# Gathering a third of the first one-hots from an identity matrix, and preparing the next stage's tiles inside the stage before it

## The reference, cut to what matters

```python
q = jnp.einsum('pd,de->pe', tb, wq).reshape(-1, PEER_HEADS, 2, half)
s = jnp.einsum('phik,hink->phin', q, subkeys).astype(jnp.float32)
s1, i1 = lax.top_k(s[:, :, 0], PEER_TOPK)
s2, i2 = lax.top_k(s[:, :, 1], PEER_TOPK)
...
gate = jax.nn.softmax(top_s, axis=-1)
ue = jnp.take(table_u, idx, axis=0)
ve = jnp.take(table_v, idx, axis=0)
act = jax.nn.gelu(jnp.einsum('pd,phkd->phk', tb, ue).astype(jnp.float32), approximate=False)
return jnp.einsum('phk,phkd->pd', (gate * act).astype(tb.dtype), ve)
```

## Time and profile before

| what | us |
|---|---|
| median of three runs | 3470.91 |
| profiled execution | 3466.3 |
| its span | 3464.5 |
| TensorE busy | 3265.2 (94%) |
| VectorE busy | 2550.3 (74%) |
| POOL busy | 557.2 (16%) |
| spreading, from the copy of chosenT to the next stage's first DMA | 2426.47 to 2628.43 |

### The profile page before, as it was taken

One profiled execution on the slowest core, in us unless ns is written; L12 is line 12 of the kernel. 1 busy time (PEld: TensorE's weight loads), 2 busy tenths in 40 slices (PEclk: granted clock), 3 DMA queues, 4 the chain that ended last, 5 costly groups with the idle time before them and its releaser, 6 DMA issues. The chain is left out here.

```text
span 3464.5 us, 48243 instructions
## 1 busy us (share of the span) xinstructions
PE 3265.2 (94%) x18404; PEld 2847.0 (82%) x18404; DVE 2550.3 (74%) x4368; ACT 1616.3 (47%) x2671; POOL 557.2 (16%) x357
## 2 busy tenths in 40 slices
PE   7997998997999999999988997999997999999997
PEld 3876997775899988888877885999886888999996
DVE  2646887254888978888883434999994887888887
ACT  4433433324565655766663324333663444444444
POOL 0211110000334420000000001555001111222220
PEclk9998999998999999999999999999998999999999
DMA  5101010342111111111114243343568998999994
GB/s 228 38 25 56 31 34 23 116 177 86 54 49 49 55 45 55 56 62 50 61 49 146 91 193 125 125 136 134 187 220 310 353 354 334 350 348 355 349 357 150
DMA packets 152468, 521.20 MB, mean 150 GB/s; under 512 B 19136, under 2 KB 66096, under 8 KB 132400
## 3 DMA queue, kind: packets, MB, share of 16 engines
q1 hardware_dynamic: 133808, 383.90, 31.1%
q0 software_dynamic: 18432, 134.23, 10.4%
HBM read 474.01 MB, written 44.06 MB: 150 GB/s over the span
## 5 line engine op out<-in xcount | busy, mean ns | idle before, releaser
L366 PE MATMUL ps<-hT_high,ring_twin 128*128 128x384 f32 (+1 forms) x1768 | 687.1, 389 | 38.2 <-DVE ring_twin L3275 17.6
L368 PE MATMUL ps<-hT_high,ring_twin 128*128 128x384 f32 (+1 forms) x1768 | 642.3, 363 | 0.0
L367 PE MATMUL ps<-hT_low,ring_twin 128*128 128x384 f32 (+1 forms) x1696 | 614.0, 362 | 0.0
L366 PEld LDWEIGHTS ps<-hT_high,ring_twin 128*128 128x128 f32 x1768 | 338.3, 191 | 86.2 <-DVE ring_twin L3275 20.2
L368 PEld LDWEIGHTS ps<-hT_high,ring_twin 128*128 128x128 f32 x1768 | 337.2, 191 | 31.6
L367 PEld LDWEIGHTS ps<-hT_low,ring_twin 128*128 128x128 f32 x1696 | 325.1, 192 | 30.7 <-issue 4.6
L366 PE MATMUL ps<-ex_vh,ex_al 128*128 128x512 f32 x768 | 301.4, 392 | 20.3 <-DVE ex_al L2812 20.3
L2331 POOL TENSOR_TENSOR pr_wl<-pr_w,pr_wh 128x1024 fp32r<-128x1024 f32 x58 | 147.2, 2540 | 997.8 <-ACT pr_wh L2390 997.8
L367 PE MATMUL ps<-ex_vl,ex_ah 128*128 128x512 f32 x768 | 301.8, 393 | 0.0
L368 PE MATMUL ps<-ex_vh,ex_ah 128*128 128x512 f32 x768 | 301.7, 393 | 0.0
L2667 POOL DMA_INDIRECT ex_uv<-in_peer_uv,rows_at x128 | 168.5, 1317 | 810.2 <-DVE ex_acc L2771 569.9
(11 more groups left out here) (610 smaller groups left out, 7690.5 us busy)
## 6 DMA issues: line engine op xcount, KB each, us to landing
ex_v<-in_peer_uv SPq DMA_DIRECT2D x128, 512.0 KB, 6.9
pr_w<-in_peer_u SPq DMA_DIRECT2D x64, 512.0 KB, 3.7
ex_u<-in_peer_u SPq DMA_DIRECT2D x64, 512.0 KB, 7.5
ring<-in_w_in_ma SPq DMA_DIRECT2D x48, 512.0 KB, 3.3
gates_by_expert<-sg_gbuf SPq DMA_DIRECT2D x6, 4096.0 KB, 15.2
ex_g<-gates_by_expert SPq DMA_DIRECT2D x32, 768.0 KB, 8.7
ring<-in_w_in_hg SPq DMA_DIRECT2D x40, 512.0 KB, 3.3
ring<-in_w_merge SPq DMA_DIRECT2D x36, 512.0 KB, 3.7
```

What stands on the lines that cost most here:

```text
L366: pe.matmul(out, a[1], b[0], start=start, stop=False)
L367: pe.matmul(out, a[0], b[1], start=False, stop=False)
L368: return pe.matmul(out, a[0], b[0], start=False, stop=stop)
```

## The change

1. `ROUTE_SHARES` ends in 12 instead of 11: 43 u tiles in the route, 21 in the spreading.
2. One ring of high and low halves (`halves`, three places) and one ring of loaded tiles (`pr_w`, four places) serve all three stages. The route halves the first two u tiles of the spreading and loads four; the spreading halves the first two v tiles of the expert stage and loads three. In the spreading, TensorE does one whole tile before its first quad. The expert stage's sum over listed rows (`acc`) lives in the fourth place of the ring.
3. The spreading loads the first three early products at its start, stores the last sixth of the gates in three pieces, and reads the first gates back (`g_first`) between them. Product stores are issued two tiles later than before (`LAG`).
4. Of every three quads from quad 5 on one is "dealt": POOL gathers its four matrices of first one-hots as rows of the identity matrix in DRAM, by the first keys, which VectorE converts to integers once, ahead of quad 2. There are 31 dealt quads, four gathers of 128 rows of 512 bytes each, and three buffers. The dealt quads have no L2533.
5. In the expert stage the third to fifth gather of rows wait for v tiles to be halved.

```diff
-ROUTE_SHARES = (4, 4, 5, 4, 5, 4, 5, 11)
+ROUTE_SHARES = (4, 4, 5, 4, 5, 4, 5, 12)
...
+SPREAD_TILES = EARLY_GROUPS * JG - ROUTE_TILES
+W_RING, H_RING = 4, 3
+SPREAD_AT = 2 * PEER_HEADS + ROUTE_TILES
+V_AT = SPREAD_AT + SPREAD_TILES
+v_place = lambda m: (V_AT + m % H_RING) % W_RING
...
+        order_next = [("u", ROUTE_TILES + n, None) for n in range(W)]
+        halved = len(order) + 2
...
+        is_dealt = lambda n: n >= 5 and n % 3 == 2
...
-        steps_to = lambda n: KD * (count - BEHIND) * n // quads
-        needed_at = lambda n: -(-quads * n // (count - BEHIND))
+        steps_to = lambda n: KD + KD * (count - BEHIND - 1) * n // quads
+        needed_at = lambda n: -(-quads * (n - 1) // (count - BEHIND - 1))
...
+                def first_gates():
+                    for b in range(2):
+                        sp.wait_ge(g_stored[b], 16 * len(range(b, N_DG - 1, 2)))
+                    sp.wait_ge(first_piece_stored, 16)
+                    sp.dma_start(g_first[:].rearrange("p t j e -> p (t j e)"),
+                                 g_dram[0].rearrange("p t e -> p (t e)")).then_inc(first_in, 16)
+
+                for m in range(H_RING):
+                    sp.dma_start(a_first[:, m, :], h_dram[m]).then_inc(first_in, 16)
...
+                last_piece(0)
+                last_piece(1)
+                first_gates()
+                last_piece(2)
+                for n in range(count + H_RING - LAG, count):
+                    store(n)
...
+            @block.gpsimd
+            def _(pool):
+                pool.wait_ge(dealt_at_ready, 1)
+                for i, n in enumerate(dealt_quads):
+                    if i >= DEALT:
+                        pool.wait_ge(g_done, dealt_quads[i - DEALT] + 1)
+                    for a in range(4):
+                        pool.indirect_dma_start(dealt[:, i % DEALT, a, :], None, d["ident"],
+                                                bass.IndirectOffsetOnAxis(ap=dealt_at[:, n, a:a + 1], axis=0)).then_inc(dealt_in[i % DEALT], 16)
...
+                    if n == 2:
+                        dve.tensor_copy(dealt_at[:], chosenT[:, 0, :].rearrange("p (q a) -> p q a", a=4)).then_inc(dealt_at_ready, 1)
+                    if not is_dealt(n):
+                        i = made_quads.index(n)
...
+                for _ in range(steps_to(0)):
+                    next(ahead, None)
...
+                    if is_dealt(n):
+                        i = dealt_quads.index(n)
+                        pe.wait_ge(dealt_in[i % DEALT], 16 * 4 * (i // DEALT + 1))
+                        hot = dealt[:, i % DEALT]
...
                     if n >= UV:
                         pool.wait_ge(row_added, n - UV + 1)
+                    elif n >= 2:
+                        pool.wait_ge(vl_ready, 2 * n - 1)
...
                     dve.wait_ge(vh_ready, m + 1)
-                    dve.tensor_tensor(vl[:, m % R, :], v[:, m % R, :], vh[:, m % R, :].bitcast(F32), ALU.subtract).then_inc(vl_ready, 1)
+                    if m < 2:
+                        dve.sem_inc(vl_ready, 1)
+                    else:
+                        dve.tensor_tensor(vl[:, vr(m), :], v(m), vh[:, vr(m), :].bitcast(F32), ALU.subtract).then_inc(vl_ready, 1)
```

More of the change, by code:

```diff
@@ L2256, in stream, with route_heads @@
             yield
-def route_heads(core, k, x, iota16, chosenT, h_dram, listed, w):
+def route_heads(core, k, x, iota16, chosenT, h_dram, listed, w, halves):
     nc, d, ps = core.nc, core.dram, k.ps
-    H, W, R, BANKS = PEER_HEADS, 4, 3, 4
+    H, W, R, BANKS = PEER_HEADS, W_RING, H_RING, 4
+    wh, wl = halves
     x_rows, rows_at, rows_gate = listed
@@ L2325, in _ @@
                     sp.wait_ge(h_stored[b], 16 * len(range(b, ROUTE_TILES, 3)))
+                for n in range(len(order), len(order) + W):
+                    sp.wait_ge(w_in[n % W], 16 * (n // W))
             @block.gpsimd
             def _(pool):
-                for n in range(len(order)):
+                for n in range(halved):
                     pool.wait_ge(high_ready, n + 1)
@@ L2384, in high @@
                 def high(n):
-                    if n < len(order):
+                    if n < halved:
                         if n >= W:
@@ L2542, in _ @@
                         made += 1
-                for n in range(made, count):
+                for n in range(made, count + 2):
                     low(n)
@@ L2552, in _ @@
                         pe.wait_ge(g_read, n - 4)
+                    if is_dealt(n):
+                        i = dealt_quads.index(n)
+                        pe.wait_ge(dealt_in[i % DEALT], 16 * 4 * (i // DEALT + 1))
+                        hot = dealt[:, i % DEALT]
+                    else:
+                        hot = one[:, made_quads.index(n) % ONE]
                     for a in range(4):
-                        t = (4 * n + a) % OH
-                        mm = pe.matmul(ps[:, 3 + n % 5, P * a:P * a + P], one[:, t, :], two[:, t, :], start=True, stop=True)
+                        mm = pe.matmul(ps[:, 3 + n % 5, P * a:P * a + P], hot[:, a, :], two[:, n % TWO, a, :], start=True, stop=True)
                     mm.then_inc(g_done, 1)
@@ L2579, in evict @@
                     act.sem_inc(h_ready, 1)
-                for n in range(R):
-                    high(n)
+                act.sem_inc(high_ready, 2)
+                high(2)
+                act.preload_act_table_set("gelu_and_others")
                 done = 0
@@ L2598, in _, with expert_sums @@
                     done += 1
-def expert_sums(core, k, x, g_dram, h_dram, listed, acc, xs, gate_row, out):
+def expert_sums(core, k, x, g_dram, h_dram, listed, w, halves, ahead, xs, gate_row, out):
     nc, d, ps = core.nc, core.dram, k.ps
-    M, E, R, UV = N_JG * JG, EARLY_GROUPS * JG, 3, 5
+    M, E, R, UV = N_JG * JG, EARLY_GROUPS * JG, H_RING, 5
+    vh, vl = halves
+    ab, g_first = ahead
+    acc = w[:, ACC_PLACE, :]
+    v = lambda m: w[:, v_place(m), :]
+    vr = lambda m: (V_AT + m) % R
     x_rows, rows_at, rows_gate = listed
@@ L2859, in experts @@
                         + [(route_w[:, n, :], row.rearrange("p k c -> p (k c)")) for n, row in enumerate(first_w)])
-        route_heads(core, k, (xh, xl), iota[:, 0:TOPK], chosenT, h_dram, listed, route_w)
-        spread_gates(core, k, (xh, xl), chosenT, iota[:], g_dram, h_dram, route_w)
+        route_heads(core, k, (xh, xl), iota[:, 0:TOPK], chosenT, h_dram, listed, route_w, halves)
+        spread_gates(core, k, (xh, xl), chosenT, iota[:], g_dram, h_dram, route_w, halves, ahead)
         route.close()
-        acc = outer.enter_context(core.sbuf("ex_acc", [P, D]))
-        expert_sums(core, k, (xh, xl), g_dram, h_dram, listed, acc, xs, rows[:, 2:4, :], out)
+        expert_sums(core, k, (xh, xl), g_dram, h_dram, listed, route_w, halves, ahead, xs, rows[:, 2:4, :], out)
 def halved(ap, size):
```

135 lines of the change are left out of this document (81 added, 54 removed).

## The result

The changed kernel takes 3491.7 us (3484.0 to 3495.1, five runs), the kernel before 3469.6 (3467.8 to 3471.6, five runs, of which the table further up has three): it takes 1.0063 times as long [1.0052, 1.0075]. The forecast was 3460, faster; it is slower by 22 us, just above the range of 3442 to 3490. The profiled execution of the changed kernel has a span of 3489.9 us.

The account below looks back on a forecast made before the run. VectorE was taken to set the spreading's pace, with stalls at the expert border; +1 (spreading, paced by POOL's gathers) + 4 (tail) - 15.5 (border) = -10.5 us gave 3460 us on the median, range 3442 to 3490.

Parts of the forecast that it names:

- Items 1 to 3 (route, VectorE, TensorE): Route one tile longer, +3.9 us; in the spreading VectorE needs 158 us, to 2588.5, and TensorE 156 us, to 2587.
- item 2: Spreading, VectorE: 31 of 96 quads lose their first one-hots, leaving 158 us, 23 less than before.
- Item 4 (POOL): Spreading: 124 gathers on POOL at 1.37 us a step set the end; last copy at 2609.3, 1 us later than before.
- the last landing: End of the spreading: the last gather's data were estimated to take 3 us to land, within 5 us after the gathers.
- X: POOL's time from one gather's start to the next in the spreading: taken as 1.37 us, bounds 1.24 and 2.1.
- rival (c): Spreading: gathers and second one-hots take turns, step 1.58 us, last copy at 2635, total 3486 us, slower; chance 0.28.
- Item 5 (tail, +4): From the spreading's last gates to the expert stage: later loads and stores cost +4 us, bounds 0 and +6.
- over 26 us after the last copy: Sign that the forecast is wrong: the next stage begins over 26 us after the spreading's last copy of gates.
- Item 6 (expert border, -15.5): Start of the expert stage: tiles halved and loaded ahead cut the loss from 21.5 to 6.0 us; bounds -19 and -8.
- 2.2 us for one low clock: Expert stage start: some eleven matmuls 0.42 us apart instead of 0.226, once, cost 2.2 us.
- 1.5 us, a guess, for the first gathered row: Expert stage start: 1.5 us allowed for the first gathered row, with al of tile 2 behind it on VectorE.
- the bound of -8: Expert border: the smallest gain allowed, if the stalls after the first matmul stay.

Follow-up runs that it names:

- e5: The changed kernel with every fourth quad gathered instead of every third, and the last quad not gathered: 3458.2 us, 0.9968 of before.
- e8: The changed kernel with a quarter gathered (not the last quad), row gathers paced, and SP's last gates ahead of the last load: 3444.3 us, 0.9927 of before.
- e3: The changed kernel with each low half one quad later on VectorE, so no first one-hot comes right behind it: 3491.4 us, 1.0067 of before.
- e4: The changed kernel without the first one-hots of undealt quads except the first three, all tensor_scalars kept: 3472.4 us.
- e6: The changed kernel without POOL's gathers in the spreading, expert row gathers starting four tiles later and paced by tiles: 3455.9 us, 0.9962 of before.
- e9: The kernel before with only the expert stage's row gathers begun later and paced by tiles: 3459.7 us, 0.9977 of before.

## Why the prediction was wrong

**Items 1 to 3 (route, VectorE, TensorE)** held as far as they can be seen. The start of the spreading moved by some 6 us between the means of the two groups of kernels, within a scatter as large; +3.9 is not contradicted. e5 and e8 show the pace of VectorE that item 2 adds up, with 96 x 1.03 + 74 x 0.60 + the low halves: 162 us worked out, 165.0 with the last quad's way to its copy.

**Item 4 (POOL) is the step that failed.** "A gather waits out the running two-input instruction once, and what VectorE begins afterwards does not hold it" gave 0.14 us of waiting and a step of 1.37 us; the step was 1.478. The 0.81 us of the earlier trace rows was right. Wrong was "once": 17 gathers met a low half, 14% of them and close to the 12% forecast, but 14 of these were held through the first one-hot behind it as well. The 17 cost 20.3 us above 0.945, where half of 1.22 us met 12% of the time makes 9.1; the 42 that met a first one-hot cost 7.4, forecast 8.9. Wrong was also that gathers meet instructions by chance: e3 takes the pairs away, and the first one-hots then cost 16.1 us. Over 123 steps the 0.108 us make 13.3 us. The second term was the last landing: from the last gather's start to the last copy's end 12.3 us passed, where X and the 5 us allowed 6.4: 5.9 more, 4.5 of them the landing itself (7.5 us for 3). Both together are 19.2 of the 19.3 us by which the spreading (197.3) was longer than forecast (2609.3 - 2431.3 = 178.0, since the first second one-hot comes 0.6 us behind 2430.7). The time is near rival (c)'s, X = 1.58 and 3486, but that is luck: its mechanism is refuted by e4 and by gathers of 0.98 us beside the second one-hots.

**Item 5 (tail, +4)** came out 2.4 us larger, just above its upper bound of 6: from the last copy to the first product on VectorE 26.6 us, 25.0 before, and that product stands at the stage's start now, 4.8 us behind it then: +6.4. The sign "over 26 us after the last copy" was met.

**Item 6 (expert border, -15.5) failed too.** The first matmul came as forecast, 2 us after the stage's start. What failed is the term behind it: 2.2 us for one low clock and "1.5 us, a guess, for the first gathered row". From 2663.1 to 2760 TensorE's starts show some 13 us lost: the pauses of 3.6 and 3.1 us, and 28 matmuls about 0.42 us apart, in three groups and not one. The wait for the first row was foreseen and mis-sized: VectorE stood 8.9 us at it, and TensorE 3.6. The later pause, for value tiles that come late (ScalarE's casts waited up to 5.3 us for them), was put at nothing. So from the last copy to the end of the span the changed kernel takes 855.2 us, 1.0 less than before, where items 5 and 6 made it 11.5 less; with the tail's +6.4 the border won some 7, about the bound of -8 that the prediction gave for stalls that stay. What bounds the start is the transfers: the pauses of the earlier trace rows were not the price of tiles that come unhalved; value tiles came late behind row gathers let go in bursts. e6 and e9 show it: with the rows later and paced the rest is 14.5 and 10.4 us shorter.

The sum was then +19.3 us for the spreading and +10.5 for the border against the forecast; with the spreading's start, 6.1 us later than forecast in this profile (2437.4 for 2431.3), that makes the 35.9 us by which the span is over it. The medians differ by 32.

## What to carry to other kernels

An engine that takes over a share of another's work must fit its step into the rhythm of the engine it helps: count how many of its pieces fit into one round of the other, with their waits, before the shares are set; here gathering a quarter made the spreading 32 us shorter than gathering a third. Where a stage starts with its queues full, loading a tile ahead only moved the stall; first look at which transfers are let go ahead of need and pace those, and at which load the first instructions of a fixed list stand waiting for.

## What was not expected of the hardware

- A POOL gather of 128 rows takes the same 0.94 to 0.98 us of POOL and 0.30 us of issue for rows of 512 bytes as for rows of 8 KB; beside the second one-hots (tensor_scalars of 128x128) it takes 0.97 us on average, beside a tensor_scalar of 128x1024 it took 1.20 and ended 0.81 us after it.
- A gather held by a two-input instruction on VectorE ends 0.82 us after it, and goes through two such instructions that follow without a gap (2.46 us).
- The data of a 64 KB gather reached TensorE 7.5 us after its end at the end of the spreading, beside a 4 MB store; the median from issue to landing over all 124 was 3.7 us.
